# The activations of the last hidden chunk carry the inverse mean square, the high parts come straight from the residual, and the last output tile goes by two groups of tokens

## What is computed

```python
x = x + merged @ w_out
h2 = rms_norm(x, g_mlp)
x = x + jnp.square(jax.nn.relu(h2 @ w_up)) @ w_down      # 1024 -> 4096 -> 1024
h3 = rms_norm(x, g_ple)
x = x + (p_l @ w_ple) * jax.nn.sigmoid(h3 @ w_ple_gate)  # p_l: 256 wide
```

## Time and profile before

| | us |
|---|---|
| median of 3 runs | 1047.34 (1046.09 to 1050.71) |
| the profiled execution | 1046.76 |
| its span in the profile | 1045.0 |
| PE busy in the span | 980.4 (94%) |
| DVE busy | 602.7 (58%) |
| ACT busy | 437.9 (42%) |

### The profile page before, as it was taken

The page is one execution under the profiler, slowest core; times in us unless marked ns, Lnnn a source line. Parts: engine busy times, 40 slices in busy tenths (PEclk is TensorE's granted clock), DMA queues, the critical chain, the costliest instruction groups (busy, mean ns, idle before and its releaser), DMA issues.

```text
span 1045.0 us, 17844 instructions
## 1 busy us (share of the span) xinstructions
PE 980.4 (94%) x7538; PEld 933.2 (89%) x7538; DVE 602.7 (58%) x816; ACT 437.9 (42%) x659; POOL 58.9 (6%) x107
## 2 busy tenths in 40 slices
PE   5798988999899999989899999999999999997996
PEld 4697977988898887989899999999999999997996
DVE  6289559840335443256566766666665665679452
ACT  6233122233544544435334734554444444434531
POOL 5000002210100004010000000000000000010000
PEclk8999998998989999999999999999999999999999
DMA  9242213470251117723222223232222233242202
GB/s 207 57 117 60 62 32 109 108 146 28 88 162 44 63 52 255 247 93 121 61 82 81 63 80 98 87 100 81 82 81 82 82 90 107 88 124 61 61 21 71
DMA packets 134416, 97.50 MB, mean 93 GB/s; under 512 B 19680, under 2 KB 124320, under 8 KB 134304
## 3 DMA queue, kind: packets, MB, share of 16 engines
q1 hardware_dynamic: 128192, 79.88, 26.2%
q0 software_dynamic: 5104, 16.47, 5.3%
q10 hardware_dynamic: 1040, 0.00, 0.1%
HBM read 86.36 MB, written 9.85 MB: 92 GB/s over the span
## 4 chain that ended last, share of the span: by engine, by line
PE 79%; DVE 8%; SPq 4%; ACT 3%; issue 3%; DMA 2%; POOL 1%; ACTq 0%; DVEq 0%; POOLq 0%
PE dense L1927 52%; PE banks L1927 19%; PE scoreA L1927 4%; PE scoreB L1927 3%; SPq L858 2%; PE banks L2042 2%; SPq L838 1%; DVE wlo L1460 1%; DVE tm L1436 1%; ACT whi L1093 1%; DMA cnat<-in_ssm_c_im 1%; DVE R L1436 1%; DVE R L1541 1%; DVE mt L1436 1%; DVE mt L1513 1%
## 5 line engine op out<-in xcount | busy, mean ns | idle before, releaser
L1460 DVE TENSOR_TENSOR wlo<-wraw,whi 128x1024 fp32r<-128x1024 f32 (+1 forms) x139 | 149.3, 1075 | 107.5 <-ACT whi L1093 93.4
L1927 PE MATMUL dense<-hid,whi 128*128 128x288 f32 x1024 | 178.6, 297 | 3.4 <-DVE R L1541 3.4
L1927 PE MATMUL dense<-act_hi,whi 128*128 128x288 f32 x736 | 165.1, 308 | 1.7 <-DVE R L1541 0.9
L1927 PE MATMUL dense<-act_hi,wlo 128*128 128x288 f32 x736 | 159.7, 300 | 0.0
L1927 PE MATMUL dense<-act_lo,whi 128*128 128x288 f32 x736 | 159.2, 300 | 0.0
L1927 PEld LDWEIGHTS dense<-hid,whi 128*128 128x128 f32 x1024 | 150.2, 188 | 3.8 <-DVE wlo L1460 3.7
L1927 PEld LDWEIGHTS dense<-act_hi,whi 128*128 128x128 f32 x736 | 120.5, 194 | 7.8 <-issue 4.8
L1093 ACT CAST whi<-wraw 128x1024 fp32r<-128x1024 f32 x100 | 104.7, 1048 | 46.2 <-PE banks L1927 44.2
L1927 PEld LDWEIGHTS dense<-act_hi,wlo 128*128 128x128 f32 x736 | 120.3, 193 | 0.0
L1927 PEld LDWEIGHTS dense<-act_lo,whi 128*128 128x128 f32 x736 | 119.8, 192 | 0.0
L1927 PE MATMUL dense<-hid,wlo 128*128 128x288 f32 x512 | 110.1, 296 | 0.0
(11 more groups left out here) (336 smaller groups left out, 1578.9 us busy)
## 6 DMA issues: line engine op xcount, KB each, us to landing
wraw<-in_w_in SPq DMA_DIRECT2D x32, 512.0 KB, 4.1
wraw<-in_w_up SPq DMA_DIRECT2D x32, 512.0 KB, 4.0
wraw<-in_w_down SPq DMA_DIRECT2D x32, 512.0 KB, 3.5
gates_spill<-gst POOLq DMA_DIRECT2D x16, 288.0 KB, 2.4
page<-in_cache_k SPq DMA_DIRECT2D x16, 256.0 KB, 3.6
page<-in_cache_v SPq DMA_DIRECT2D x16, 256.0 KB, 6.4
wraw<-in_w_out SPq DMA_DIRECT2D x8, 512.0 KB, 4.0
wraw<-in_w_ple_gate SPq DMA_DIRECT2D x8, 512.0 KB, 3.8
```

What stands on the lines that cost most here:

```text
L1460: return nc.vector.tensor_tensor(out=lo, in0=whole, in1=f32(hi), op=ALU.subtract)
L1927: return nc.tensor.matmul(out, lhsT, rhs, start=start, stop=stop, skip_group_check=True)
```

## The change

1. In the events of hidden tiles 28 to 31 (chunk 7), DVE multiplies `hs` by `inv` between ACT's square and ACT's rounding. ACT waits for it.
2. `R` is multiplied by `inv` in the down units of chunk 6, and no more in those of chunk 7.
3. The event `inv` stands ahead of pair (20, 21) and not after the last pair. Its loads of `p` on POOL stay where they were (now event `pload`).
4. `xf` is gone. ACT makes `act_hi` from `R` with the gain as its scale, once DVE has released the PSUM buffer, and DVE makes `act_lo` in one instruction, `R` times gain minus `act_hi`. This holds at both feeds.
5. The last pgate unit runs in two groups of tokens: first the 24 matmuls of tokens 0 to 255, then the transposes of tile 6, then the 24 matmuls of tokens 256 to 575; each group has its own chain of DVE, ACT, DVE, DVE. Then TensorE transposes the first group, then the second.
6. The second half of the columns is stored without the last tile once tile 6 is ready (5 transfers of 384 columns), and the last 128 columns by three more transfers: one for each two blocks of 128 tokens (SP), and the samples' (issued by ACT, after a copy by DVE).

```diff
@@ schedule_of
     for m in range(FIRSTPAIR, 32, 2):
+        if m == LASTHID - 8:
+            event("inv")
         pair()
-    event("inv")
+    event("pload")
...
-    for m in range(KT + 1):
-        if m < KT:
-            unit()
+    for m in range(KT - 1):
+        unit()
         if m:
             event("yout", m - 1)
...
+    flush()
+    event("last", 0)
+    event("yout", KT - 2)
...
+    event("last", 1)
...
+    for part in range(2):
+        event("lastout", part)
@@ SP
-            for part in range(2):
-                sync.wait_ge(*read(("yout", KT // 2 * (part + 1) - 1, "b")))
-                cols = slice(D // 2 * part, D // 2 * part + D // 2)
+            for upto, cols in ((3, slice(0, D // 2)), (KT - 2, slice(D // 2, D - P))):
+                sync.wait_ge(*read(("yout", upto, "b")))
...
+            for part in range(2):
+                sync.wait_ge(last_act, part + 1)
+                sync.dma_start(yp[256 * part:256 * part + 256, D - P:D].rearrange("(t p) c -> p t c", p=P),
+                               ytok[:, 2 * part:2 * part + 2, D - P:D]).then_inc(y_stored, 16)
@@ ACT, feed and hidden
-            def feed(m, w):
-                scalar.wait_ge(xf_ready, count.next(xf_ready))
-                nc.scalar.copy(act[0][:, m, :], xf[:, m % 2, :]).then_inc(count.up(act_hi), 1)
+            def feed(m, w, job):
+                scalar.wait_ge(*read(job))
+                nc.scalar.activation(act[0][:, m, :], R[:, m, :], ACT.Copy, scale=gains[:, w, m:m + 1]).then_inc(
+                    count.up(act_hi), 1)
...
+                if m < LASTHID:
...
+                else:
+                    nc.scalar.activation(hs[:, m % 2, :], hr[:, m % 2, :], ACT.Square).then_inc(count.up(hs_ready), 1)
+                    scalar.wait_ge(hs_scaled, m - LASTHID + 1)
@@ ACT, the end
+                elif k == "lastout":
+                    part = a[0]
+                    scalar.wait_ge(last_turned, part + 1)
+                    nc.scalar.copy(ytok[:, 2 * part:2 * part + 2, D - P:D], ...).then_inc(count.up(last_act), 1)
+                    if part:
+                        scalar.wait_ge(last_dve, 1)
+                        scalar.dma_start(o["y_sample"].rearrange("b s d -> (b s) d")[:, D - P:D], ytok[0:TS, 4, D - P:D])...
@@ DVE
-            def feed(m, w):
-                vector.wait_ge(*count.last)
-                nc.vector.tensor_scalar(xf[:, m % 2, :], R[:, m, :], gains[:, w, m:m + 1], None, ALU.mult)...
             def feed_low(m, w):
                 vector.wait_ge(act_hi, KT * (w - 1) + m + 1)
-                lower(act[1][:, m, :], xf[:, m % 2, :], act[0][:, m, :]).then_inc(count.up(act_lo), 1)
+                nc.vector.scalar_tensor_tensor(out=act[1][:, m, :], in0=R[:, m, :], scalar=gains[:, w, m:m + 1],
+                                               in1=f32(act[0][:, m, :]), op0=ALU.mult, op1=ALU.subtract)...
...
-                        if m // 8 == 7:
+                        if m // 8 == 6:
                             vector.wait_ge(*count.last)
                             tt(R[:, m % 8, :], R[:, m % 8, :], inv[:], ALU.mult).then_inc(count.up(dve_steps), 1)
...
+                elif k == "hid" and sum(a) >= LASTHID:
+                    m = sum(a)
+                    vector.wait_ge(hs_ready, m - LASTHID + 1)
+                    tt(hs[:, m % 2, :], hs[:, m % 2, :], inv[:], ALU.mult).then_inc(count.up(hs_scaled), 1)
@@ PE
+            def last_unit(part):
...
+                out = dplace(job)[:, part, 0:c1 - c0]
+                for k in range(KT):
+                    ins = three(out, [w[:, k, :] for w in (wh, wl)], [x[:, k, c0:c1] for x in act],
+                                start=k == 0, stop=k == KT - 1)
+                ins.then_inc(last_full, 1)
```

More of the change, by code:

```diff
@@ L1047, in _ @@
                         load_x2(t)
-                elif k == "inv":
+                elif k == "pload":
                     pool.wait_ge(p_full, 7 * NPAIR)
@@ L1184, in unit_out @@
                     elif kind == "out":
-                        feed(m, 1)
+                        feed(m, 1, job)
                     elif kind == "down" and m0 // 8 == 7:
-                        feed(m % 8, 2)
+                        feed(m % 8, 2, job)
                     elif kind == "ple":
@@ L1194, in unit_out @@
                             count.up(ysg_ready), 1)
+            def last_unit(part):
+                c0, c1 = LASTCUT[part]
+                scalar.wait_ge(last_gate, part + 1)
+                nc.scalar.activation(ysg[:, 1, c0:c1], yf[:, 1, c0:c1], ACT.Sigmoid).then_inc(count.up(ysg_ready), 1)
             nc.scalar.preload_act_table_set("sqrt_and_others")
@@ L1557, in unit_out @@
                 if kind == "down" and m0 // 8 == 7:
-                    for j in range(nm):
-                        feed((m0 + j) % 8, 2)
                     for j in range(nm):
@@ L1913, in _ @@
                         count.up(hid_lo), 1)
+                elif k == "last":
+                    part, m = a[0], KT - 1
+                    c0, c1 = LASTCUT[part]
+                    y = yf[:, 1, c0:c1]
+                    if part == 0:
+                        vector.wait_ge(last_full, 1)
+                        vector.wait_ge(*full(("yout", m - 2, "b")))
+                    else:
+                        vector.wait_ge(last_full, 2)
+                    tt(y, inv[:, c0:c1], dplace(("m", len(units) - 1, 0))[:, part, 0:c1 - c0], ALU.mult).then_inc(
+                        count.up(last_gate), 1)
+                    vector.wait_ge(ysg_ready, count.next(ysg_ready))
+                    tt(y, ysg[:, 1, c0:c1], pw[:, m, c0:c1], ALU.mult).then_inc(count.up(dve_steps), 1)
+                    vector.wait_ge(*count.last)
+                    tt(y, y, R[:, m, c0:c1], ALU.add).then_inc(count.up(yf_ready), 1)
+                elif k == "lastout" and a[0] == 1:
+                    vector.wait_ge(last_turned, 3)
+                    nc.vector.tensor_copy(ytok[0:TS, 4, D - P:D], banks[0:TS, 3, 0:P]).then_inc(count.up(last_dve), 1)
                 elif k == "pT":
@@ L2010, in unit, with last_unit @@
                         ins.then_inc(full_of(job), 1)
+            def last_unit(part):
+                u = len(units) - 1
+                job = ("m", u, 0)
+                c0, c1 = LASTCUT[part]
+                if part == 0:
+                    tensor.wait_ge(w_lo, turn["split", u])
+                    tensor.wait_ge(*free(job))
+                wh, wl = [wview(w, wslot(u), u) for w in (whi, wlo)]
+                out = dplace(job)[:, part, 0:c1 - c0]
[3 more added lines that the diff above has]
+                ins.then_inc(last_full, 1)
             def product(u, j):
@@ L2360, in _ @@
                     ins.then_inc(full_of(e), 1)
+                elif k == "last":
+                    last_unit(a[0])
+                elif k == "lastout":
+                    part = a[0]
+                    tensor.wait_ge(yf_ready, KT + part)
+                    if part == 0:
+                        for ab in "ab":
+                            tensor.wait_ge(*read(("ms", 1, ab)))
+                    for t in range(2):
+                        c0 = 256 * part + P * t
+                        ins = transpose(banks[:, part, P * t:P * t + P], yf[:, 1, c0:c0 + P])
+                    ins.then_inc(last_turned, 1)
+                    if part:
+                        tensor.wait_ge(*read(("yout", KT - 2, "b")))
+                        transpose(banks[0:TS, 3, 0:P], yf[:, 1, TP:T]).then_inc(last_turned, 1)
                 elif k == "yout":
```

35 lines of the change are left out of this document (27 added, 8 removed).

## The result

| | before | after |
|---|---|---|
| median, us | 1048.88 (4 runs, 1046.09 to 1050.71) | 1034.7 (4 runs, 1032.83 to 1035.88) |
| the profiled execution | 1046.76 | 1035.88 |
| its span | 1045.0 | 1034.2 |
| PE busy in the span | 980.4 | 981.4 |
| DVE busy | 602.7 | 598.3 |

The ratio is 0.9876, with a 95% interval of 0.9853 to 0.9898: faster by 1.0 to 1.5%. The forecast was 1034.8.

What follows compares the result with a forecast made beforehand. DVE was taken to bound the end of chunk 7, plus a late tail. 9.8 - 0.1 + 2.8 = 12.5 us off the profiled 1046.76 gives 1034.3, plus 0.58 for the median: 1034.8; range 1032.0 to 1040.5.

Steps and rivals of the forecast that it cites:

- Part 1: Chunk 7: with less DVE load, PE's waits on the split and most of that on pw go; gain 9.8 us.
- All three terms: Chunk 7: 5.4 us of split waits, the 3.4 us wait on pw shrunk to 0.5, and 1.5 us of slow clock.
- slow stretch: After the wait on pw, 17 matmuls at granted clock 0.55 lost 1.5 us; claimed to vanish with a short wait.
- 5.8 us of DVE against PE's 6.41: Chunk 7 units: after the change each asks 5.8 us of DVE, under PE's 6.41, so the three split waits go.
- Part 2: Pair stage: takes over the reciprocal and 12 multiplications; hand-overs just use up the slack; charge 0.1 us, between 0 and 3.2.
- D: Rival, pair stage: all four hand-overs come through in full, costing 3.2 us; total gain 9.4, 1037.9 us; chance 0.07.
- Part 3: Feed of the out units: DVE is relieved there too, but PE's waits are not on act_lo; no gain.
- Part 4: Tail: shorter last chain and fewer late store issues move the end by 2.8 us; bounds 0.9 and 3.6.
- the upper bound: Tail: 3.6 us gained if the smaller pieces land after 2.0 us instead of 2.9.
- B: Rival, end of chunk 7: ACT takes DVE's place, the 3.4 us wait and slow stretch stay; gain 8.1, 1039.2 us; chance 0.12.
- C: Rival, tail: a slow landing, not the chain, sets the end; gain 10.6, 1036.7 us; chance 0.08.
- E: Rival, gate: new PE waits keep the clock low there; slower than before, 1069 us if all 384 matmuls; chance 0.03.

Runs made afterwards that it cites:

- e12: Changed kernel with two unused 576-column multiplications on DVE added at the end of each chunk 7 unit; chunk 7 41.85 us, ratio to before 0.9887.
- e4: Kernel before with the new tail alone (divided last unit, last 128 columns stored apart); tail 61.64 us, ratio to before 0.9957.
- e2: Kernel before with the new feed alone (no xf), reciprocal and multiplications of R kept in chunk 7; chunk 7 43.15 us, ratio to before 0.9914.
- e6: Changed kernel with the old tail and the multiplications by inv back on R in chunk 7, reciprocal still early; chunk 7 42.30 us, ratio to before 0.9943.
- e10: Changed kernel with two unused squares of R on ACT ahead of the first copy to pw; chunk 7 41.65 us, ratio to before 0.9883.
- e13: Changed kernel with three unused squares of R on ACT ahead of the first copy to pw; chunk 7 42.21 us, ratio to before 0.9898.
- e1: Kernel before with the norm's scaling and reciprocal moved, xf and the old tail kept; chunk 7 44.23 us, ratio to before 0.9931.
- e3: Changed kernel with the old tail (undivided last unit, old stores); chunk 7 40.49 us, tail 65.18, ratio to before 0.9898.
- e5: Changed kernel with the last unit undivided but the last 128 columns stored apart; tail 63.24 us, ratio to before 0.9899.
- e8: Changed kernel with the last unit cut at column 384 in place of 256; tail 61.21 us, ratio to before 0.9883.

## Why the prediction was right, and where it was not

**Part 1, 9.8 us: measured 9.75.** All three terms came: no wait on `wlo`, 0.5 us left on `pw`, no slow stretch. The matmul of `sqsum` starts 7.2 us earlier (972.71 for 979.90), 9.4 if the 2.25 us are taken off by which the 96 start late. `act_lo` took 0.811 (taken: 0.80) and `act_hi` 0.778 (0.77). The step "5.8 us of DVE against PE's 6.41" is what e12 tests from the other side: with 1.5 us more in a unit PE waits again (0.42 and 0.24 us). What the prediction didn't see is that its two causes overlap. The norm alone gives 6.0 and the feed alone 7.1, 13.1 together, and both give 9.75, since each frees some of the same waits and the feed alone already loses the slow stretch.

**The slow stretch, 1.5 us: right outcome, a reason that doesn't hold.** I had argued that waits up to 1.9 us leave the clock alone and the one of 3.4 lowers it. PE's waits in these stretches and the granted clock of the 3.8 us behind: 1.48, 1.66, 1.75 (before), 1.49 (e4), 1.57 (e2), 1.59 (e6), 1.65 (e10), 2.22 (e13): 1.00. 1.75 (e4): 0.57; 1.80 (e1): 0.55; 3.19 (before): 0.55; 3.20 (e4): 0.69. The same 1.75 us stands on both sides, and 2.22 on the harmless one. Nor does the fall follow the wait at a fixed distance: in before the clock is at 0.50 from 968.8 on, 0.3 us after the wait of 3.19 has ended; in e4, after the one of 3.20, it is 1.00 until 970.4 and 0.50 from 970.5 on, 1.4 us after its end. What decides isn't settled. Behind waits of about 0.5 us there was no slow stretch in any of the five traces that have one (after, e3, e5, e8 and e12: 9.85 to 9.87 us for the 72 matmuls). The Trainium skill ("TensorE: Matmul & The Clock Gate", section "A second HAM failure mode: psum-queue depth-cycling") says of another kernel that frequent short idling between groups of matmuls makes the clock swing. e1 and e4, with their waits in the units before, fit it, and e13, with one longer wait alone, too; but e2, e12 and before have such waits and kept 1.00 behind most of them. It names a risk here, not a condition.

**Part 2, 0.1 us: measured 0.31.** The reciprocal ahead of pair (20, 21) cost nothing (e6: 324.95 against 324.96), and the loss is in all kernels that scale `hs` and in no other (e1 0.28). The prediction had the add end with the slack just used up, at 899.1 on the clock of before; the trace is 2.25 us later at this place (pair (28, 29) starts at 883.92 where it was 881.67), and on that clock the add ends at 899.12 and PE starts at 899.27, not 899.10. So the add was timed right, and what was too small was what it costs once there is no slack: 0.2 us there and 0.1 in pair (30, 31). D's 3.2 us didn't come.

**Part 3, nothing: nothing.** From the first matmul of the out units (on `mg`) to the first of the 96 are 93.1, 94.1 and 93.2 us with the old feed (before, e1, e4) and 92.9, 93.8 and 92.9 with the new (after, e2, e3): no gain that stands out of the 1 us by which they scatter.

**Part 4, 2.8 us: measured 3.6.** The chain was sized right: from DVE's start to the transposes 2.10 us (2.05 in the sum), from there to the last issue 0.90 (0.9). The mis-sized term is the landing, taken as 3.17 us after the last issue as in before: it was 2.49. The last transfer of before, the samples' 128 KB, took 2.8 us to land; the last pieces, 128 KB of the prompt twice and 32 KB of the samples, took 1.8 to 2.0. The 3.6 us are the upper bound that I had named and not chosen; from the last group's DVE start to the end of the span are 5.5 us, where 6.2 were forecast. (Redone from rows 10 and 11 the two bounds are 2.8 + 2.9 - 2.0 = 3.7 and 2.8 - 4.6 + 2.9 = 1.1; the range doesn't hang on it.) The Trainium skill ("DMA: Bandwidth & Descriptors", section "Bandwidth") would have let the pieces save nothing, by its rule to batch; e5, which against e3 does nothing but cut the stores, gained 1.9 us. Its rule is on bandwidth, and what ended this kernel was the last transfer's time to land and the issues in line before it.

**The sum** was 12.5 us and the stages measured 13.05. That the forecast of 1034.8 met 1034.7 to a tenth is luck: the median of before rose by 1.5 us with one more run, and the profiled execution of after was 2.4 us late before it reached the change (514.06 for 511.65). Rivals B, C and E can be read off as not come: the wait on `pw` is 0.5, the last transfer lands 2.0 us after its issue (the span ends 2.5 after it), and the clock is 1.00 to the end of the last unit.

## What to carry to other kernels

Where an engine off the matrix path is busy for nearly all of a stretch (31.0 of 32.1 us here) and the matrix engine shows waits, count its load per unit against the matrix engine's time per unit: under it the waits go, over it they come back after the lead is used up, and two cures for the same stretch give less together than the sum of what each gives alone (9.75 us for 6.0 and 7.1). Behind such a stretch look at what the next engine has in its queue after the last result; here one split of 0.95 us ahead of a copy of 0.54 was the whole wait that was left. For the end of a kernel, shorten the last chain and the line of issues behind it: here storing the other columns early and leaving two transfers for the end, in place of five, gave 1.9 us. Don't count on matmuls of under 256 columns being faster (112 ns at 192, 117 at 256). And compare by stages when code that no edit touched moves the total by more than the edits do.

## What the runs showed of the hardware that I had not expected

- Matmuls between weight loads of 128 columns (190 ns, pipelined) follow each other every 177 ns at 384 columns, 147 at 320, 133.5 at 288, 117 at 256 and 112 at 192 columns: from 256 to 192 hardly anything is gained.
- A granted clock of 0.55 to 0.57 for 3.8 us came after PE waits of 1.75 and 1.80 us in two executions, and didn't after 1.75 and 2.22 us in two others.
- Transfers of the prompt's output landed the sooner the smaller they were, and the length of their rows made no difference that shows: 256 KB in 2.4 to 2.5 us, be the rows 2 KB long or 512 bytes (e5's last), 192 KB in 2.1 with rows of 1.5 KB or 512 bytes (e8), 128 KB in 1.8 to 1.9 and 64 KB in 1.6 (e8), both with rows of 512 bytes. Those of the samples, 64 rows each, are slower for their size: 128 KB in 2.8, 96 KB in 2.1 and 32 KB in 1.9 to 2.1, from SP and from ACT alike.
- A scalar_tensor_tensor of 576 columns in SBUF takes 0.811 us where a tensor_tensor takes 0.756.
